# A two-layer streaming encoder on one core: turns between sub-layers by token halves, x on VectorE alone, bias inside the ada dot products

## The chip, the core and the metric

The kernel runs on one core of a Trainium2 chip. The metric is the device time of one execution in microseconds. Three timed runs stand for the kernel before, and one further execution was recorded by the hardware profiler; all durations below come from that one.

## What is computed

544 tokens of width 1024 (512 of a new stream, 32 of a running one) pass through two layers. Each layer has three sub-layers, j = 0, 1, 2: a half-step SwiGLU feed-forward part, a mixer (latent attention beside retention, with one input and one output projection), and a second feed-forward part. Every sub-layer is wrapped in the same way:

```python
mods = silu(c) @ ada_w[l] + ada_b[l]            # 9 vectors of 1024 per layer and stream
h = rms_norm(x, g_pre) * (1 + mods[scale]) + mods[shift]
o = sublayer(h)                                 # swiglu(h @ w1, h @ w3) @ w2, or mixer(h) @ w_out
x = x + coef * mods[gate] * rms_norm(o, g_post) # coef 0.5, 1, 0.5
```

Both norms run over the 1024 features of each token. The outputs are x after both layers, and the new caches and retention states.

## The kernel before

**Layout.** Activations lie feature-major: x is eight rows m = 0 to 7 of 128 features (one per partition) by 544 tokens. A token half is 272 columns, the width of one PSUM bank's use; pair(b) is both halves in banks b and b+1. Every matmul of a projection is done three times with operands split into a high and a low fp32r part: w_hi·h_hi, w_hi·h_lo and w_lo·h_hi (tile3, L668).

**Weights.** SyncE loads a weight chunk into one of two slots of raw, ScalarE casts it to w_hi (high, L1127, and high_at), GpSimd (POOL) subtracts to get w_lo (low, L539), TensorE uses both and counts w_used. A chunk is 1024 columns, or 1408 in the down projection of a feed-forward part, where one output tile needs two chunks (22 k-steps) and there are eight output tiles. The mixer's output tile needs one chunk (8 k-steps). A chunk's cast waits until the chunk two before it, which had the same slot, has been used.

**The ada dot products.** During a down projection VectorE computes mods for the next sub-layers: one tensor_tensor_reduce per tile of 128 outputs and stream (ada_group, L1470), with the tile of ada_w in one of four slots of SBUF and c spread over PSUM banks 4 to 7 (c_psum). There are 48 tiles in a layer's first feed-forward part and 24 in the second (8 in the last layer's), four to a group; a group ends with two additions of the bias (L1486). SyncE's one queue issues these tiles in turn with the down chunks, and each waits for a dot product that frees its slot.

**A turn.** Between two sub-layers each engine's program does this, in order:

- ScalarE, out_tiles (L1225): squares each output tile from PSUM (L1239) and copies it, scaled by gate and gain, to o_buf (L1248, L1250). POOL adds the squares of the tiles up to the seventh (add_square, L545).
- TensorE, at the end of out_tiles: token_sums (L689) multiplies the squares by ones for five groups of tokens, so that each token's sum lies on its own partition; ScalarE takes the root (L1146), VectorE the reciprocal (L1509), TensorE spreads it over all partitions with five transposes (spread, L695).
- VectorE, turn_over (L1504): for each row m a product o·inverse (L1516) and the addition to x (L1520). The additions of rows 1, 3 and 5 are left to POOL (add_odd, L565).
- ScalarE, pre_scale (L1149): h_hi = cast of x·scale for each row (L1157), in two pieces, one for each stream, with the squares of x (L1167) three rows behind. POOL adds the squares of rows 0 to 3.
- VectorE: h_lo for each row (L1550), behind all of x.
- TensorE, first_tiles (L703): the first two output tiles (w = 0, 1) of the next sub-layer. For each row k as it arrives it does the two high products of both tiles and both token halves, 8 matmuls; then, for each w, the products with h_lo, with the sums of squares of x between them (add_squares, L685; five of them).

The order on every engine is written out by hand; semaphores count the steps (x_prod, x_new, h_high, h_ready, sums, sq_added, rooted, inverted, inv_spread, columns, ada_done). At the end of the program the turn has only its first half, and SyncE stores each row of y as x_new counts it (L528). At the start the first turn has only its second half, and takes x from DMA.

## Time and profile before

| | |
|---|---|
| timed runs | median 2369.93 us, 2367.03 to 2370.04 (3 runs) |
| profiled execution | 2367.46 us |
| its span | 2365.7 us |
| TensorE (PE) busy | 2298.3 us |
| VectorE (DVE) busy | 1217.7 us |
| ScalarE (ACT) busy | 807.0 us |
| POOL busy | 907.6 us |
| chain of waits | PE 71%, issue 14%, DVE 8%, DMA 2%, POOL 2%, ACT 1% |

The span runs from the first to the last recorded instruction; the profiled execution's own time is 1.76 us longer. Busy shares are averages over the whole span. Nearly all of it is TensorE streaming through projections; the turns are short stretches in which TensorE's idle time shows only if the profile is asked for that stretch. Starts in a timeline are microseconds from the start of the span. A row with several instructions (x4) gives the time from the first's start to the last's end.

### The profile page before, as it was taken

The page shows a single profiled execution, that of the slowest core. Times are in us where ns is not written, and L with a number is a line of the kernel's source. Part 1 is how long each engine was busy: PE and PEld are TensorE (multiplying, and loading weights), DVE is VectorE, ACT ScalarE, POOL GpSimd, SP SyncE. Part 2 cuts the span into 40 slices and gives each one's busy share as a digit, 9 for nine tenths or more (in the row PEclk, how much of TensorE's full clock was granted, in tenths as well). Part 3 has the DMA queues.
Part 4 walks back from the last instruction along what each step waited for, and adds up shares of the span by engine and source line. Part 5 has one row for each costly group of instructions (what it writes and reads, how often), then busy time and mean ns, then how long its engine had stood idle before and what let it go on. Part 6 is the DMA issues. An engine that isn't in the chain of part 4 may idle for free.

```text
span 2365.7 us, 43949 instructions
## 1 busy us (share of the span) xinstructions
PE 2298.3 (97%) x17664; PEld 2180.3 (92%) x17664; DVE 1217.7 (51%) x2017; ACT 807.0 (34%) x1332; POOL 907.6 (38%) x400
## 2 busy tenths in 40 slices
PE   7999999999999999999999999998999999999997
PEld 7999999899558899999989999998994699999997
DVE  6333379877561533337153333997846524333501
ACT  3322332333454422332242333224343543333321
POOL 2334444434113434434444443444421153443353
PEclk8999999999999999999999999999999999999998
DMA  6222268422211122237212223872231022222421
GB/s 233 89 89 86 83 238 297 143 90 80 73 37 54 63 89 84 85 128 250 103 63 85 83 89 124 279 271 94 81 111 51 1 72 79 82 88 89 162 94 66
DMA packets 70934, 263.62 MB, mean 111 GB/s; under 512 B 8704, under 2 KB 10112, under 8 KB 70336
## 3 DMA queue, kind: packets, MB, share of 16 engines
q1 hardware_dynamic: 70848, 262.44, 32.3%
q8 instruction: 59, 0.97, 0.2%
q14 instruction: 27, 0.22, 0.0%
HBM read 258.96 MB, written 3.45 MB: 111 GB/s over the span
## 4 chain that ended last, share of the span: by engine, by line
PE 71%; issue 14%; DVE 8%; DMA 2%; POOL 2%; ACT 1%; SPq 1%; DVEq 0%; POOLq 0%; ACTq 0%
PE ps L679 20%; PE ps L675 20%; PE ps L676 20%; DVE wide_v L1481 2%; POOL w_lo L542 2%; DMA ada_w<-in_ada 2%; PE ps L685 1%; DVE wide_v L1516 1%; PE ps L725 1%; DVE h_lo L1550 1%; PE ps L1046 1%; DVE x L1520 1%; PE ps L931 1%; DMA x<-in_x 1%; PE ps L1013 1%
## 5 line engine op out<-in xcount | busy, mean ns | idle before, releaser
L542 POOL TENSOR_TENSOR w_lo<-raw,w_hi 128x1024 fp32r<-128x1024 f32 (+1 forms) x304 | 785.2, 2583 | 1278.3 <-ACT w_hi L1139 947.1
L675 PE MATMUL ps<-h_hi,w_hi 128*128 128x272 f32 x3296 | 887.1, 289 | 3.8 <-POOL w_lo L542 3.8
L676 PE MATMUL ps<-h_lo,w_hi 128*128 128x272 f32 x3296 | 889.3, 287 | 0.0
L679 PE MATMUL ps<-h_hi,w_lo 128*128 128x272 f32 x3296 | 685.6, 289 | 0.0
L675 PEld LDWEIGHTS ps<-h_hi,w_hi 128*128 128x128 f32 x3296 | 619.1, 188 | 5.2 <-POOL w_lo L542 5.1
L676 PEld LDWEIGHTS ps<-h_lo,w_hi 128*128 128x128 f32 x3296 | 620.9, 188 | 0.2
L1139 ACT CAST w_hi<-raw 128x1024 fp32r<-128x1024 f32 (+1 forms) x236 | 268.4, 1137 | 831.9 <-PE ps L679 773.9
L679 PEld LDWEIGHTS ps<-h_hi,w_lo 128*128 128x128 f32 x3296 | 519.1, 188 | 0.0
L675 PE MATMUL ps<-u_hi,w_hi 128*128 128x272 f32 x1408 | 380.1, 288 | 0.0
L676 PE MATMUL ps<-u_lo,w_hi 128*128 128x272 f32 x1408 | 379.9, 289 | 0.0
L1481 DVE CUSTOM_DVE_ANT_0 wide_v<-ada_w,ps 128x1024 bf16<-128x1024 f32 x256 | 295.1, 1217 | 27.5 <-DMA ada_w<-in_ada 15.0
L679 PE MATMUL ps<-u_hi,w_lo 128*128 128x272 f32 x1408 | 291.6, 288 | 0.0
L1568 DVE TENSOR_TENSOR wide_v<-ps,rinv 128x544 f32<-128x544 f32 x88 | 63.7, 724 | 437.3 <-PE ps L679 437.3
L675 PEld LDWEIGHTS ps<-u_hi,w_hi 128*128 128x128 f32 x1408 | 264.8, 188 | 0.7 <-POOL w_lo L542 0.7
L676 PEld LDWEIGHTS ps<-u_lo,w_hi 128*128 128x128 f32 x1408 | 265.2, 188 | 0.0
L1573 DVE SCALAR_TENSOR_TENSOR wide_v<-wide_v,wide_s 128x512 f32<-128x512 f32 (+1 forms) x176 | 193.9, 1140 | 104.7 <-ACT wide_s L1211 104.7
L679 PEld LDWEIGHTS ps<-u_hi,w_lo 128*128 128x128 f32 x1408 | 220.3, 188 | 0.0
L1509 DVE RECIPROCAL tok_inv<-tok_root 128x5 f32<-128x5 f32 x6 | 1.1, 188 | 260.8 <-ACT tok_root L1146 260.8
L1214 ACT CAST u_hi<-wide_v 128x544 f32 (+1 forms) x88 | 56.9, 647 | 213.7 <-DVE wide_v L1573 213.7
L1132 ACT CAST w_hi<-raw 128x1024 fp32r<-128x1024 f32 x68 | 71.0, 1045 | 143.6 <-PE ps L679 88.2
L1578 DVE TENSOR_TENSOR u_lo<-wide_v,u_hi 128x544 f32 x88 | 63.9, 726 | 80.1 <-ACT u_hi L1214 80.1
L1211 ACT ACTIVATE wide_s<-wide_s 128x512 f32<-128x512 f32 (+1 forms) x176 | 81.9, 513 | 4.6 <-DVE wide_s L1565 4.6
(257 smaller groups left out, 2390.7 us busy)
## 6 DMA issues: line engine op xcount, KB each, us to landing
raw<-in_w_up SPq DMA_DIRECT2D x176, 512.0 KB, 3.3
ada_w<-in_ada SPq DMA_DIRECT2D x128, 512.0 KB, 4.7
raw<-in_w_dn SPq DMA_DIRECT2D x64, 704.0 KB, 5.4
raw<-in_w_mix SPq DMA_DIRECT2D x64, 512.0 KB, 3.4
ada_first<-in_ada SPq DMA_DIRECT2D x10, 512.0 KB, 7.8
decay<-in_decay SPq DMA_DIRECT2D x2, 2048.0 KB, 10.0
ada_first<-in_ada_first SPq DMA_DIRECT2D x6, 512.0 KB, 11.3
x<-in_x SPq DMA_DIRECT2D x4, 544.0 KB, 16.9
```

The costliest lines, as they stand in the source:

```text
L542: pool.tensor_tensor(w_lo[:, slot, 0:width], raw[:, slot, 0:width], w_hi[:, slot, 0:width].bitcast(F32), ALU.subtract).then_inc(lo_done.se ...
L675: pe.matmul(ps[:, bank + t, 0:width[t]], wh, hi[:, n], start=start, stop=False)
L676: pe.matmul(ps[:, bank + t, 0:width[t]], wh, lo[:, n], start=False, stop=False)
L679: last = pe.matmul(ps[:, bank + t, 0:width[t]], wl, hi[:, n], start=False, stop=stop)
L1132: nc.scalar.copy(w_hi[:, slot, 0:width], raw[:, slot, 0:width]).then_inc(hi_done.sem, 1)
L1139: nc.scalar.copy(w_hi[:, k, 0:width], raw[:, k, 0:width]).then_inc(hi_done.sem, 1)
L1211: nc.scalar.activation(wide_s[:, f, at], wide_s[:, f, at], ACT.Silu, bias=wide_s[:, f, T + 2 * v:T + 2 * v + 1]).then_inc(up_silu.sem, 1)
L1214: nc.scalar.copy(u_hi[:, bass.ds(i * 2 + f, 1), :].rearrange("p a n -> p (a n)"), tmp_v[:, f, :]).then_inc(up_hi.sem, 1)
L1481: v_.tensor_tensor_reduce(junk[v], ada_w[:, t, :], c_psum(v), 1.0, 0.0, ALU.mult, ALU.add, acc[:, buf, v, t:t + 1]).then_inc(ada_done.sem, 1)
L1568: v_.tensor_tensor(halves(tmp_v[:, f, :]), pair(4 * f + 2), halves(rinv[:, :]), ALU.mult)
L1573: v_.scalar_tensor_tensor(out=wide_v[:, f, at], in0=wide_v[:, f, at], scalar=wide_v[:, f, T + 2 * v:T + 2 * v + 1], in1=wide_s[:, f, at], ...
L1578: v_.tensor_tensor(u_lo[:, at, :].rearrange("p a n -> p (a n)"), tmp_v[:, f, :], u_hi[:, at, :].rearrange("p a n -> p (a n)").bitcast(F32) ...
```

## The change

The turns are rewritten.

- **Last output tile.** In every out_tiles the last tile is now done by last_tile: all k-steps of the first 272 tokens, then all of the second 272. Within the second half, at k = 2 TensorE makes the first half's column sums (half_sums(0)), at k = 6 it spreads the first half's inverse (spread(0)). The sums wait for ada_done there. The second half's sums and spread lie in the next sub-layer's first_tiles, within w = 0.
- **x after a feed-forward part** (j = 0, 2). VectorE makes the first token half of all eight rows and then the second. Products go to PSUM banks 6 and 7 instead of SBUF. Nothing is left to POOL.
- **x after the mixer** (j = 1). VectorE makes it in whole rows, products in PSUM banks 6 and 7, each row waiting for the one before.
- **ScalarE.** scaled() takes a token half. After a feed-forward part five rows of the first half are scaled before the last tile's second half is read; the cast of the next chunk stands between. After the mixer both halves of a row follow each other.
- **first_tiles.** The high products of the first token half come first, all rows for w = 0, then all for w = 1; then the second half, row by row, for both.
- **ada.** The dots' loop is written out; the bias is the accumulator's initial value and the result goes straight to mods. The two bias additions per group are gone; columns no longer counts groups.
- **Start.** The first turn scales all rows' first half, then all rows' second.

```diff
...
-TOK_AT = [0, P, 2 * P, 3 * P, T - P]
+TOK_AT = [0, P, HT - P]
 TOK = len(TOK_AT)
...
-SUMS = KD - N_EARLY + 2
+SUMS = KD - N_EARLY + 3
...
-            def add_odd(l, j, m):
-
-                pool.wait_ge(x_prod.sem, x_prod.at(l, j * KD + m + 1))
-                pool.tensor_tensor(x[:, m, :], x[:, m, :], tmp_v[:, 1, :], ALU.add).then_inc(x_new[1].sem, 1)
...
+            def half_sums(l, j, t):
+
+                if t == 0:
+                    pe.wait_ge(sq_added.sem, sq_added.at(l, (j + 1) * SQ))
+                    if j != 1:
+                        pe.wait_ge(ada_done.sem, ada_done.at(
+                            l, 2 * (ADA_A if j == 0 else ADA_A + (ADA_B if l < DEPTH - 1 else KD))))
+                token_sums(squares[:, :], t, True, False)
+                if t:
+                    pe.wait_ge(out_sq.sem, out_sq.at(l, (j + 1) * KD))
+                else:
+                    pe.wait_ge(half_sq.sem, half_sq.at(l, j + 1))
+                token_sums(tmp_s[:, 1, :], t, False, True).then_inc(sums.sem, 1)
+
+            def spread(l, j, t):
+
+                pe.wait_ge(inverted.sem, inverted.at(l, 3 * j + 2 + t))
+                for b in range(2):
+                    c = t * TOK + b
+                    pe.transpose(ps[:, 4 + t, b * P:(b + 1) * P], tok_inv[:, c:c + 1].to_broadcast([P, P]), ident[:, :])
+                c = t * TOK + 2
+                pe.transpose(ps[:, 4 + t, HT - NS:HT], tok_inv[P - NS:P, c:c + 1].to_broadcast([NS, P]),
                              ident[P - NS:P, P - NS:P]).then_inc(inv_spread.sem, 1)
 
...
+                for w in range(2 if l or j else 0):
+                    pe.wait_ge(lo_done.sem, lo_done.at(l, chunk + w + 1))
+                    for k in range(KD):
+                        if w == 0 and k == (0 if j == 2 else 1):
+                            half_sums(*post, 1)
+                        if w == 0 and k == (0 if j == 2 else 5):
+                            spread(*post, 1)
+                        if w == 0:
+                            pe.wait_ge(h_high.sem, h_high.at(l, high_count(l, j, 0, k)))
+                        pe.matmul(ps[:, 2 * w, 0:HT], w_hi[:, w, k * P:(k + 1) * P], h_hi[:, k, 0:HT],
+                                  start=k == 0, stop=False)
+                        pe.matmul(ps[:, 2 * w, 0:HT], w_lo[:, w, k * P:(k + 1) * P], h_hi[:, k, 0:HT],
+                                  start=False, stop=False)
                 for k in range(KD if l or j else 0):
-                    pe.wait_ge(h_high.sem, h_high.at(l, high_count(l, j, k)))
+                    pe.wait_ge(h_high.sem, h_high.at(l, high_count(l, j, 1, k)))
                     for w in range(2):
...
+                        pe.matmul(ps[:, 2 * w + 1, 0:HB], w_hi[:, w, k * P:(k + 1) * P], h_hi[:, k, HT:HT + HB],
+                                  start=k == 0, stop=False)
+                        pe.matmul(ps[:, 2 * w + 1, 0:HB], w_lo[:, w, k * P:(k + 1) * P], h_hi[:, k, HT:HT + HB],
+                                  start=False, stop=False)
...
+            def last_tile(l, j, chunk0, per_tile, chunk_tiles, operand):
+
+                pe.wait_ge(out_ev.sem, out_ev.at(l, j * KD + KD - 2))
+                n0 = chunk0 + (KD - 1) * per_tile
+                last_k = per_tile * chunk_tiles - 1
+                for t in range(2):
+                    n = slice(t * HT, (t + 1) * HT)
+                    for q in range(per_tile):
+                        if t == 0:
+                            pe.wait_ge(lo_done.sem, lo_done.at(l, n0 + q + 1))
+                        for kk in range(chunk_tiles):
+                            k = q * chunk_tiles + kk
+                            if t and k == 2:
+                                half_sums(l, j, 0)
+                            if t and k == 6:
+                                spread(l, j, 0)
+                            hi, lo = operand(k)
+                            slot = (n0 + q) % 2
+                            wh, wl = (w[:, slot, kk * P:(kk + 1) * P] for w in (w_hi, w_lo))
+                            pe.matmul(ps[:, 2 + t, 0:HT], wh, hi[:, n], start=k == 0, stop=False)
+                            pe.matmul(ps[:, 2 + t, 0:HT], wh, lo[:, n], start=False, stop=False)
+                            last = pe.matmul(ps[:, 2 + t, 0:HT], wl, hi[:, n], start=False, stop=k == last_k)
+                        if t:
+                            last.then_inc(w_used.sem, 1)
+                    if t == 0:
+                        last.then_inc(half_mm.sem, 1)
+                if l == DEPTH - 1 and j == 2:
+                    half_sums(l, j, 1)
+                    spread(l, j, 1)
...
+            def scaled(l, j, t, m):
+
+                if l or j:
+                    act.wait_ge(x_new.sem, x_new.at(l, x_count(j - 1, t, m)))
+                elif t == 0:
+                    act.wait_ge(x_in[m // 2].sem, 16)
+                for v, n in ((0, slice(HT, NP_)), (1, slice(NP_, T))) if t else ((0, slice(0, HT)),):
+                    nc.scalar.activation(h_hi[:, m, n], x[:, m, n], ACT.Copy, scale=mul_pre[:, j, v, m:m + 1])\
+                        .then_inc(h_high.sem, 1)
+
...
+            def last_tile(l, j, chunk0, per_tile, o_buf, pre):
+
+                in_u = per_tile == 2
+                ahead = 5 if in_u else 0
+                if pre is not None:
+                    pre_l, pre_j, chunk = pre
+                act.wait_ge(half_mm.sem, half_mm.at(l, j + 1))
+                act.wait_ge(sq_added.sem, sq_added.at(l, j * SQ + N_EARLY + KD - 2))
+                nc.scalar.activation(tmp_s[:, 1, 0:HT], ps[:, 2, 0:HT], ACT.Square).then_inc(half_sq.sem, 1)
+                act.wait_ge(columns.sem, columns.at(l, (2, COL_A, COL_A + 2)[j]))
+                nc.scalar.activation(o_buf[:, KD - 1, 0:HT], ps[:, 2, 0:HT], ACT.Copy,
+                                     scale=mul_post[:, j, 0, KD - 1:KD]).then_inc(half_ev.sem, 1)
+                act.wait_ge(sums.sem, sums.at(l, (j + 1) * SUMS - 1))
+                token_root(0)
+                if pre is not None:
+                    high(pre_l, chunk, 0, KD * P)
+                    if in_u:
+                        shift_columns(pre_l, pre_j)
+                        for m in range(ahead):
+                            scaled(pre_l, pre_j, 0, m)
+
+                act.wait_ge(w_used.sem, w_used.at(l, chunk0 + KD * per_tile))
+                nc.scalar.activation(tmp_s[:, 1, HT:T], ps[:, 3, 0:HT], ACT.Square).then_inc(out_sq.sem, 1)
+                if pre is not None and in_u:
+                    high(pre_l, chunk + 1, 1, KD * P)
+                if pre is not None and not in_u:
+                    shift_columns(pre_l, pre_j)
+                act.wait_ge(sums.sem, sums.at(l, (j + 1) * SUMS))
+                token_root(1)
+                if pre is not None and not in_u:
+                    high(pre_l, chunk + 1, 1, KD * P)
+                n = NP_ - HT
+                nc.scalar.activation(o_buf[:, KD - 1, HT:NP_], ps[:, 3, 0:n], ACT.Copy,
+                                     scale=mul_post[:, j, 0, KD - 1:KD])
+                nc.scalar.activation(o_buf[:, KD - 1, NP_:T], ps[:, 3, n:HT], ACT.Copy,
+                                     scale=mul_post[:, j, 1, KD - 1:KD]).then_inc(out_ev.sem, 1)
+                if pre is not None:
+                    for m in range(ahead, KD if in_u else 0):
+                        scaled(pre_l, pre_j, 0, m)
+                    pre_scale(pre_l, pre_j, chunk)
...
+                        if j == 2:
+                            scaled(l, j, 0, m)
+                        scaled(l, j, 1, m)
...
-            def ada_group(l, buf, land_n, n0, done0, cols, first_ffn=False):
+            def ada_group(l, land_n, n0, done0, first_ffn=False):
+                b0 = l * MODS + 16 + done0
 
                 for t in range(ADA_RING):
                     dve.wait_ge(ada_landed[t].sem, ada_landed[t].at(l, land_n * 16 + 16))
                     if t == 0:
-                        dve.wait_ge(columns.sem, columns.at(l, cols - 2))
-
                         dve.wait_ge(up_lo.sem, up_lo.at(l, FT if first_ffn else 2 * FT))
                         dve.wait_ge(c_placed.sem, c_placed.at(l, 1 if first_ffn else 2))
                     for v in range(2):
                         dve.wait_ge(ada_done.sem, ada_done.at(l, 2 * done0 + (2 * t + v - 1)))
-                        v_.tensor_tensor_reduce(junk[v], ada_w[:, t, :], c_psum(v), 1.0, 0.0, ALU.mult,
-                                                ALU.add, acc[:, buf, v, t:t + 1]).then_inc(ada_done.sem, 1)
-                dve.wait_ge(ada_done.sem, ada_done.at(l, 2 * done0 + 2 * ADA_RING))
-                for v in range(2):
-                    bias = ada_b[:, bass.ds(l * MODS + 16 + done0, ADA_RING)]
-                    v_.tensor_tensor(mods[:, v, bass.ds(n0, ADA_RING)], acc[:, buf, v, :], bias, ALU.add)\
-                        .then_inc(columns.sem, 1)
+                        v_.tensor_tensor_reduce(junk[v], ada_w[:, t, :], c_psum(v), 1.0,
+                                                ada_b[:, b0 + t:b0 + t + 1], ALU.mult, ALU.add,
+                                                mods[:, v, n0 + t:n0 + t + 1]).then_inc(ada_done.sem, 1)
...
+                    def invert(t):
+                        dve.wait_ge(rooted.sem, rooted.at(l, 3 * j + 2 + t))
+                        n = slice(t * TOK, (t + 1) * TOK)
+                        v_.reciprocal(tok_inv[:, n], tok_root[:, n]).then_inc(inverted.sem, 1)
+
+                    if j == 1:
+                        for t in range(2):
+                            invert(t)
+                        dve.wait_ge(inv_spread.sem, inv_spread.at(l, 2 * j + 2))
+                        for m in range(KD):
+                            dve.wait_ge(out_ev.sem, out_ev.at(l, j * KD + m + 1))
+                            c = x_count(j, 1, m)
+                            if m:
+                                dve.wait_ge(x_new.sem, x_new.at(l, c - 1))
+                            v_.tensor_tensor(pair(6), halves(o_buf[:, m, 0:T]), pair(4), ALU.mult).then_inc(x_prod.sem, 1)
+                            dve.wait_ge(x_prod.sem, x_prod.at(l, c))
+                            v_.tensor_tensor(halves(x[:, m, 0:T]), halves(x[:, m, 0:T]), pair(6), ALU.add)\
+                                .then_inc(x_new.sem, 1)
+                    for t in range(2 if j != 1 else 0):
+                        n = slice(t * HT, (t + 1) * HT)
+                        invert(t)
+                        dve.wait_ge(inv_spread.sem, inv_spread.at(l, 2 * j + t + 1))
+                        for m in range(KD):
+                            if t == 0 and m == KD - 1:
+                                dve.wait_ge(half_ev.sem, half_ev.at(l, j + 1))
+                            else:
+                                dve.wait_ge(out_ev.sem, out_ev.at(l, j * KD + m + 1))
+                            c = x_count(j, t, m)
+                            prod = ps[:, 6 + m % 2, 0:HT]
+                            if t or m >= 2:
+
+                                dve.wait_ge(x_new.sem, x_new.at(l, c - 2))
+                            v_.tensor_tensor(prod, o_buf[:, m, n], ps[:, 4 + t, 0:HT], ALU.mult).then_inc(x_prod.sem, 1)
+                            dve.wait_ge(x_prod.sem, x_prod.at(l, c))
+                            v_.tensor_tensor(x[:, m, n], x[:, m, n], prod, ALU.add).then_inc(x_new.sem, 1)
```

## Rows read from the trace of the kernel before

**Rows 1.** The page, busy time by engine: us, share of span, instructions.
```profile
PE 2298.3 (97%) x17664; PEld 2180.3 (92%) x17664; DVE 1217.7 (51%) x2017; ACT 807.0 (34%) x1332; POOL 907.6 (38%) x400
```

**Rows 2.** Waits of TensorE: line, released by, us in total, times, longest.
```profile
PE ps L715 <- ACT h_hi L1157: 9.2, 7, 2.5
...
PE ps L692 <- DVE acc L1481: 2.6, 2, 1.3
```

**Rows 3.** Stretches: start:end, length, each engine's busy us, granted clock, DMA share, GB/s.
```profile
425.30:472.90 47.60, 41.72 (x274) 38.37 (x272) 41.55 (x73) 20.28 (x40) 20.78 (x11) 0.89 0.34 119
767.30:801.60 34.30, 30.25 (x191) 27.76 (x191) 21.26 (x33) 18.91 (x39) 17.59 (x10) 0.90 0.12 39
1171.50:1216.30 44.80, 40.26 (x276) 37.54 (x275) 21.23 (x33) 20.28 (x40) 20.80 (x11) 0.92 0.11 36
1586.50:1632.90 46.40, 40.29 (x273) 37.29 (x272) 41.39 (x73) 20.30 (x40) 20.77 (x11) 0.93 0.35 123
1927.50:1962.20 34.70, 30.66 (x191) 27.97 (x190) 21.23 (x33) 18.91 (x39) 17.58 (x10) 0.85 0.11 37
2332.20:2365.70 33.50, 19.66 (x159) 19.30 (x157) 10.76 (x14) 4.59 (x10) 8.53 (x5) 0.80 0.17 67
```

**Rows 4.** Timeline of VectorE, turn of 1171.5: start, us, instruction, idle before it.
```profile
1191.90 0.72 DVE L1516 TENSOR_TENSOR wide_v<-o_ffn,ps 128x544 f32<-128x544 f32 x1 [0.91 <-PE ps L701]
1192.65 0.72 DVE L1520 TENSOR_TENSOR x<-x,wide_v 128x544 f32<-128x544 f32 x1
...
1201.97 1.14 DVE L1520 TENSOR_TENSOR x<-x,wide_v 128x544 f32<-128x544 f32 x1
...
1203.20 8.88 DVE L1550 SCALAR_TENSOR_TENSOR h_lo<-x,mul_pre,h_hi 128x512 fp32r<-128x512 f32 x16
```

**Rows 5.** Timeline of TensorE, at a tile's start and in the mixer's turn.
```profile
425.34 0.29 PE L675 MATMUL ps<-u_hi,w_hi 128*128 128x272 f32 x1
425.47 0.29 PE L676 MATMUL ps<-u_lo,w_hi 128*128 128x272 f32 x1
...
779.72 0.57 PE L715 MATMUL ps<-h_hi,w_hi 128*128 128x272 f32 x1 [2.58 <-issue]
...
785.31 0.43 PE L717 MATMUL ps<-h_hi,w_lo 128*128 128x276 f32 x1
785.54 0.34 PE L715 MATMUL ps<-h_hi,w_hi 128*128 128x272 f32 x1
...
791.85 0.41 PE L725 MATMUL ps<-h_lo,w_hi 128*128 128x272 f32 x2
```

**Rows 6.** Timeline of ScalarE and POOL: cast and split of chunk 15.
```profile
425.29 1.37 ACT L1139 CAST w_hi<-raw 128x1408 fp32r<-128x1408 f32 x1 [6.91 <-PE ps L679]
426.74 3.24 POOL L542 TENSOR_TENSOR w_lo<-raw,w_hi 128x1408 fp32r<-128x1408 f32 x1 [5.05 <-ACT w_hi L1139]
```

**Rows 7.** Timeline of VectorE in a mixer: 256 columns, one operand in PSUM.
```profile
634.39 0.36 DVE L1711 TENSOR_TENSOR ret_st<-ps,decay 128x256 f32<-128x256 f32 x1
634.67 0.94 DVE L1719 RECIPROCAL ret_root<-ret_root 128x128 f32<-128x128 f32 x1
```

**Rows 8.** Groups of ScalarE by form: count, busy us, mean ns, idle before.
```profile
L1157 ACT ACTIVATE h_hi<-x,mul_pre 128x512 fp32r<-128x512 f32 x48 | 34.2, 713 | 27.2 <-POOL x L568 10.0 <-DVE x L1520 9.2 <-DVE mul_pre L1492 5.5
L1157 ACT ACTIVATE h_hi<-x,mul_pre 128x32 fp32r<-128x32 f32 x48 | 14.7, 306 | 0.0
```

**Rows 9.** Timeline of VectorE: the first dot, then the last group of dots.
```profile
317.18 1.22 DVE L1481 CUSTOM_DVE_ANT_0 wide_v<-ada_w,ps 128x1024 bf16<-128x1024 f32 x1 [1.16 <-ACT ps L1263]
...
433.78 1.22 DVE L1481 CUSTOM_DVE_ANT_0 wide_v<-ada_w,ps 128x1024 bf16<-128x1024 f32 x1 [0.30 <-DVE mods L1486]
...
442.92 0.08 DVE L1481 DVE_READ_ACCUMULATOR2_ANT acc<- 128x1 f32 x1
```

**Rows 10.** The page, DMA issues: queue, count, KB each, median us to landing.
```profile
ada_w<-in_ada SPq DMA_DIRECT2D x128, 512.0 KB, 4.7
...
out_y<-x SPq DMA_DIRECT2D x8, 272.0 KB, 2.1
```

More of the change, by code:

```diff
@@ L277, in streaming_trunk @@
         c_placed = signal("c_placed", 2)
-        x_prod = signal("x_prod", 24)
-        x_new = [signal(f"x_new{i}", 12, 4) for i in range(2)]
+        x_prod = signal("x_prod", 40)
+        x_new = signal("x_new", 40)
         x_sq = signal("x_sq", 24)
@@ L573, in turn_over @@
                     low(l, chunk + k, k, KD * P)
-                if l or j:
-                    for m in range(1, KD - 1, 2):
-                        add_odd(*((l, j - 1) if j else (l - 1, 2)), m)
                 for m in range(1, N_EARLY):
@@ L620, in _ @@
                 ffn(l, 1)
-            for m in range(1, KD - 1, 2):
-                add_odd(DEPTH - 1, 2, m)
         @block.tensor
@@ L687, in add_squares, with token_sums @@
                 return last
-            def token_sums(src, bank, start, stop):
+            def token_sums(src, t, start, stop):
                 for b, at in enumerate(TOK_AT):
-                    last = pe.matmul(by_token(bank)[:, b:b + 1], src[:, at:at + P], ones[:, 0:1],
+                    last = pe.matmul(by_token(t)[:, b:b + 1], src[:, t * HT + at:t * HT + at + P], ones[:, 0:1],
                                      start=start and b == 0, stop=stop, skip_group_check=True)
                 return last
-            def spread(l, n, bank):
-                pe.wait_ge(inverted.sem, inverted.at(l, 2 * n + 2))
-                for b in range(4):
-                    pe.transpose(ps[:, bank, b * P:(b + 1) * P], tok_inv[:, b:b + 1].to_broadcast([P, P]), ident[:, :])
-                pe.transpose(ps[:, bank + 1, 0:NS], tok_inv[P - NS:P, 4:5].to_broadcast([NS, P]),
+            def half_sums(l, j, t):
[10 more added lines that the diff above has]
+                token_sums(tmp_s[:, 1, :], t, False, True).then_inc(sums.sem, 1)
@@ L795, in out_tiles @@
-                pe.wait_ge(out_sq.sem, out_sq.at(l, (j + 1) * KD))
-                token_sums(tmp_s[:, 1, :], 4, False, True).then_inc(sums.sem, 1)
-                spread(l, j, 4)
+                tile(KD - 2, 0, False)
+                last_tile(l, j, chunk0, per_tile, chunk_tiles, operand)
+            def last_tile(l, j, chunk0, per_tile, chunk_tiles, operand):
[26 more added lines that the diff above has]
+                    spread(l, j, 1)
@@ new lines, in shift_columns @@
+            def shift_columns(l, j):
+                act.wait_ge(columns.sem, columns.at(l, COL_A if j else 0))
+                for v in range(2):
+                    c = 3 * j * KD
+                    nc.scalar.copy(h_hi[:, :, T + 2 * v:T + 2 * v + 2],
+                                   mods[:, v, c:c + KD].unsqueeze(2).to_broadcast([P, KD, 2])).then_inc(h_high.sem, 1)
+            def last_tile(l, j, chunk0, per_tile, o_buf, pre):
[36 more added lines that the diff above has]
+                    pre_scale(pre_l, pre_j, chunk)
@@ L1187, in pre_scale @@
                     act.wait_ge(columns.sem, 6)
-                    for m in range(KD):
-                        scaled(m)
-                    shift_columns()
+                    for t in range(2):
+                        for m in range(KD):
+                            scaled(l, j, t, m)
+                    shift_columns(l, j)
                     act.wait_ge(ada_done.sem, 2 * FIRST_TILES)
@@ new lines, in turn_over @@
+                    if j == 1:
+                        for t in range(2):
+                            invert(t)
[9 more added lines that the diff above has]
+                                .then_inc(x_new.sem, 1)
@@ L1833, in mixer @@
                 heads_low(len(ITEMS) - 1)
-            for k in range(KD):
-                v_.memset(scratch[:, 4 + k:5 + k], 0.0).then_inc(x_new[k % 2].sem, 1)
             for v in range(2):
```

165 lines of the change are left out of this document (61 added, 104 removed).

## The prediction

> **What bounds the kernel now.** The page comes first: its busy shares give TensorE 97% of the span [rows 1], so only two things can move the time, TensorE's own work and the places where it stands still. The list of waits, asked for TensorE, says where: at L715 for the scaled activations (ScalarE), at L692 for the ada dot products (VectorE), 2.6 us in two waits [rows 2]. Both lie where one sub-layer's output becomes the next one's input, which I call a turn. There are five between sub-layers and a half one at the end. The table of stretches gives each, from the first matmul of the last output tile to the last matmul of the next sub-layer's first two tiles [rows 3]: 47.6 and 46.4 us for feed-forward to mixer, 34.3 and 34.7 for mixer to feed-forward, 44.8 for feed-forward to the next layer, and 33.5 from the last output tile to the end of the span. TensorE's busy time is 4 to 6 us short of the stretch in each of the five and 14 short in the last, and its clock is below 1.00 in all.
>
> Inside a turn VectorE's timeline shows the order. In the turn of 1171.5 the products and sums that make x run from 1191.90 to 1203.11, then the low parts of h take 8.9 us [rows 4], and TensorE's part on the low parts trails them. That last part of TensorE is 9.8 us long (791.85 [rows 5] to the end of the mixer's turn, 801.6 [rows 3]). So the path is: x on VectorE, h_lo on VectorE, TensorE's last part. I count everything below from the start of the last output tile, as +t.
>
> **Feed-forward turns (three).** The last output tile is 22 k-steps of 6 matmuls, which at full clock follow each other every 0.125 us [rows 5]: 16.5 us. Its first token half now comes first, and needs the second weight chunk after 4.1 us instead of 8.3. That chunk's cast and split take 1.37 and 3.24 us from +0.2 on [rows 6]: it is there at +4.8, 0.7 late. The half ends at +9.1. Two k-steps into the second half TensorE makes six column sums, ScalarE the root, VectorE the reciprocal; at k = 6 TensorE spreads it, until +12.6. The sums are no new work but the old 20 and 5 transposes cut into 12 and 6. The tile ends at +18.6 (before +16.5).
>
> VectorE starts x's first half there, at +12.6. No row has 272 columns with a PSUM destination. The nearest has 256 with a PSUM operand: 0.36 us, the next instruction 0.28 behind it [rows 7]. I take 0.30 for the product and 0.41 for the sum, which waits for it: 0.71 a row, 5.7 us a half, done at +18.3. TensorE sums and spreads the second half by +21.4 (ScalarE casts a chunk in between), so x is whole at +27.1; before it was at +31.6 (1203.11).
>
> Meanwhile TensorE works on the first half of h: w = 0 until +22.5, w = 1 until +24.5. ScalarE scales the second half in two pieces per row and squares whole rows. A 512-column scale is busy for 0.71 and a 32-column one for 0.31 [rows 8]; they overlap by about 0.1, so I take 0.57 for 240 plus 32 columns, 0.38 for 272 and 0.55 for a square. With POOL's three additions between, the last row is scaled at +30.5: ScalarE is last here, not VectorE. TensorE starts on the low parts at +31.0 (before 44.8 - 9.8, +35.0), VectorE has finished them at +36.3, and the turn is through at +40.5. With half operations of 0.36 and 0.46 it is +41.4. I take +40.9: the turns gain 6.7, 5.5 and 3.9 us, 16.1 together.
>
> A rule of the Trainium skill speaks against halving; it stands outside this sum. VectorE: DVE Perf Modes, section on the TRN2 errata, charges every instruction a fixed latency, 120 cycles beside one per element when the source is in PSUM. The 256-column row (0.36 us) has such a fixed part but is shorter. By an estimate from that page a half operation is 0.41 us, and all turns together gain some 3 us less.
>
> **The ada dots.** TensorE's first column sums write a bank that the dots read, so they wait for all dots. Before, they came at +16.5 and waited 1.3 us twice. Now they come at +9.8; the old finish is +17.9 (442.92 + 0.08 [rows 9]). The change takes the bias additions out and unrolls the loop. Eight dots and eight accumulator reads take 9.14 us (433.78 to 442.92), so 96 take 109.7; from 317.18 to 443.00 they took 125.8, and the other 16 us are gaps at 12 group ends. Without gaps VectorE alone would finish at +1.8. But then the queue sets the pace: a down chunk goes out only when the chunk two before it is split, 8.3 us apart, with three ada tiles behind each. With a landing of 4.7 us [rows 10] the last dots are done at +8.2, 1.6 us ahead of need. The column multipliers follow on VectorE and can touch the first reciprocal. The bounds are 0 and +8.1 us in each of two turns; I take 0.5 each, as hardly an old group shows idle time but at its end.
>
> **Mixer turns (two).** The tile is 8 k-steps, 6.0 us; with the interruptions it ends at +7.4. TensorE waits for the next chunk's split (its 1024 columns take 1024/1408 of the cast and split of [rows 6]; +8.3), sums the second half, spreads by +10.3, and only then VectorE makes x in whole rows. Both operations of a row wait for the one before, 0.75 us from start to start [rows 4]: 1.5 us a row, whole at +22.3 against about +21.1. What costs is the new order of first_tiles. TensorE takes the first half of h for w = 0 over all eight rows before anything else, 2 matmuls per 1.5 us, and when the last row is ready (+23.5) 50 of 64 matmuls are still to do, 6.2 us at full clock, to +29.8. Before, each row brought 8 matmuls, and all were done at 791.85 (+24.5). VectorE's low parts (+31.5) hide nothing of it, as TensorE's last part takes 9.2 us more: +39.0, 4.6 worse than before.
>
> The clock comes on top. In the old turn, after 2.6 us without work, matmuls followed each other 0.23 us apart from 779.72 to 785.54, the 1.2 GHz level, and then at 2.4 [rows 5]. In the new one TensorE idles for over two thirds of every row until +23.5, so the burst begins low. If that lasts 5.8 us as there, it costs 0.45 of it, 2.6 us (1 - 0.125/0.227); if the level has come back, nothing. I take 1.6: +40.6, or 6.3 and 5.9 us worse, 12.2 together (bounds 9 and 14.2).
>
> The Trainium skill, TensorE: Matmul & The Clock Gate, section "What's actually happening", has the low level as the default that only activity releases. The old row agrees: 0.23 us apart after the idling. By that rule the burst pays its whole bound, and the sum is 2 us worse.
>
> **The ends.** At the end the second half's sums follow the tile (+18.6), products start at +21.0, the last row is ready at +26.7, and its DMA lands 2.1 us later [rows 10], with 0.5 for eight rows close together: +29.3 against +33.5. Gain 4.2; bounds 2.5 and 4.5. At the start ScalarE scales 24 pieces, 7.4 us, instead of 16, 6.6 us, and the squares wait for it: 0.75 worse, or 0 if a DMA hides it.
>
> **Sum.** -16.1 + 1.0 + 12.2 - 4.2 + 0.75 = -6.4 us. The profiled execution took 2367.46, 1.76 beyond its span, so it gives 2361.1. The three timed runs have a median of 2369.93, 2.5 above it. Midway I expect 2362.
>
> **Rivals.**
> (a) Better: the clock is full when the mixer's burst comes (-3.2), half operations run at 0.28 and 0.36 (-2), no ada wait (-1): 2355. For it: the pitch of 0.28 exists. Against: TensorE's thin work just before the burst.
> (b) Half operations as slow as 0.42 and 0.55, because PSUM is written and read back. Feed-forward turns 42.6, the end 2 us longer, the mixer's x 2 us later each: +5 +2 +4, so 2372, no gain. For it: no row has VectorE writing PSUM. Against: those reading it cost nothing extra (0.36).
> (c) Slower: TensorE waits at the half's sums for the ada dots, two k-steps into the second half of the last tile, twice. It decides from +9.8 on. If landings, not gaps, set the dots' pace, they still end at +17.9, each such turn at +48.6, and the time is 2376. For it: 4.7 us of landing in a ring of four, behind larger chunks on one queue. Against: dots follow each other every 1.14 us within the old groups.
> (d) The bias edit does only half of what it says (the unrolled code brings stalls of its own): dots end at +13.8, +4 us each, 2369, no difference.
>
> **How the numbers follow.** A change under 0.2% (4.7 us) cannot be told from none. Forecast (2357 to 2367) 0.50, (a) 0.13, (b) 0.12, (c) 0.15, (d) 0.10. Faster means below 2365.2: four fifths of the forecast's case, (a) and a little of the rest: 0.60. Slower: (c) and the tail of (b), 0.16. Within: the rest, 0.24. The range runs from (a)'s 2354 to 2372, at (b), and leaves (c) out.
>
> **What would show it.** In the new trace: half operations of x at 0.3 to 0.4 us; feed-forward turns of 40 to 42 us; the last dot before +9.8 and no wait of TensorE for it; mixer turns of 39 to 42 us with the clock low beyond +23.5. I am wrong if the mixer turns are no longer than before, if ada waits of several us stand in two turns, or if the feed-forward turns shrink by less than 3 us.

## The result, and the profile after

The change makes the kernel slower: 2378.53 us (median of 14 runs) against 2369.98 (14 runs), ratio 1.0033 with a 95% interval of 1.0026 to 1.0040. The forecast was 2362. The profiled execution took 2376.92 us; its span is 2375.1, 9.4 more than before. The page gives TensorE the same share as before [rows 1]:

```profile
PE 2306.4 (97%) x17694; PEld 2184.5 (92%) x17694; DVE 1214.2 (51%) x2033; ACT 821.2 (35%) x1392; POOL 880.8 (37%) x382
```

The stretches of the changed kernel, cut as in [rows 3]: three feed-forward turns, two mixer turns and the end, in their order in time.

```profile
427.90:472.00 44.10, 41.54 (x281) 38.75 (x280) 33.00 (x75) 22.42 (x50) 16.05 (x8) 0.92 0.26 90
767.80:809.70 41.90, 32.42 (x196) 28.61 (x195) 21.34 (x37) 21.05 (x49) 12.93 (x7) 0.80 0.10 31
1180.00:1223.60 43.60, 40.47 (x281) 37.40 (x280) 23.91 (x53) 22.41 (x50) 16.05 (x8) 0.96 0.12 37
1593.80:1636.90 43.10, 40.14 (x280) 37.46 (x279) 33.23 (x75) 22.41 (x50) 16.06 (x8) 0.96 0.26 92
1931.30:1973.40 42.10, 32.61 (x196) 28.81 (x195) 21.33 (x37) 21.05 (x49) 12.93 (x7) 0.80 0.09 33
2343.70:2375.10 31.40, 20.85 (x164) 20.04 (x162) 13.34 (x34) 5.04 (x12) 4.51 (x2) 0.86 0.19 72
```

Set against the lengths of [rows 3] and the terms of the prediction's sum:

| term | predicted | in the trace |
|---|---|---|
| start (first last-tile at 427.9, before 425.3) | +0.75 | +2.6 |
| three feed-forward turns | -16.1 | -3.5, -1.2, -3.3 = -8.0 |
| wait for the dots | +1.0 | 0 |
| two mixer turns | +12.2 | +7.6, +7.4 = +15.0 |
| end | -4.2 | -2.1 |
| between the turns | 0 | +1.9 |
| sum | -6.4 | +9.4 |

The last column compares one profiled execution of each kernel. Every turn moved the way that was forecast, but nearly every size is off, and all but one (the wait for the dots) to the slow side. TensorE's waits (line waited for, released by, us, times, longest) show where:

```profile
PE ps L730 <- ACT h_hi L1203: 16.1, 16, 2.1
PE ps L737 <- ACT h_hi L1203: 6.7, 11, 1.4
...
PE ps L688 <- POOL w_lo L548: 1.8, 2, 0.9
```

L730 is the first token half's high product in first_tiles: 8 of its 16 waits lie in each mixer turn, one per row. No wait for the dots is left [rows 2]: the last dot ends 8.6 us into the first turn (forecast +8.2), 1.3 us before the column sums that need it (+9.9), though each now takes 1.20 us from start to start instead of 1.14 [rows 9]. VectorE at the last dot:

```profile
435.16 1.30 DVE L1563 CUSTOM_DVE_ANT_0 wide_v<-ada_w,ps,ada_b 128x1024 bf16<-128x1024 f32 x1
436.36 0.11 DVE L1563 DVE_READ_ACCUMULATOR2_ANT mods<- 128x1 f32 x1
```

**A feed-forward turn.** From VectorE's timeline in the first turn: product, sum and next product of x's second half, then the low parts.

```profile
450.46 0.45 DVE L1618 TENSOR_TENSOR ps<-o_ffn,ps 128x272 f32<-128x272 f32 x1 [1.02 <-PE ps L713]
450.94 0.44 DVE L1620 TENSOR_TENSOR x<-x,ps 128x272 f32<-128x272 f32 x1
451.29 0.44 DVE L1618 TENSOR_TENSOR ps<-o_ffn,ps 128x272 f32<-128x272 f32 x1
...
457.84 8.86 DVE L1649 SCALAR_TENSOR_TENSOR h_lo<-x,mul_pre,h_hi 128x512 fp32r<-128x512 f32 x16
```

An operation behind an unrelated one starts 0.35 us after it, the sum behind its own product 0.48: 0.83 a row (forecast 0.71), 6.7 us a half. x is whole at +29.3 (forecast +27.1), h_lo done at 466.70, +38.8 (+36.3). The last row is scaled at +32.3 (460.24; forecast +30.5):

```profile
459.55 0.69 ACT L1203 ACTIVATE h_hi<-x,mul_pre 128x240 fp32r<-128x240 f32 x2
```

**A mixer turn.** TensorE's granted clock is the column behind POOL's busy time:

```profile
781.00:793.20 12.20, 5.75 (x14) 3.51 (x14) 11.25 (x17) 10.32 (x27) 4.00 (x4) 0.50 0.14 45
793.20:796.40 3.20, 3.16 (x14) 3.16 (x15) 3.20 (x7) 1.80 (x4) 1.42 (x1) 0.50 0.00 0
796.40:801.10 4.70, 4.70 (x38) 4.70 (x38) 4.05 (x10) 0.00 (x0) 0.00 (x0) 0.99 0.00 0
801.10:809.70 8.60, 8.60 (x54) 7.80 (x53) 1.04 (x1) 3.09 (x4) 2.39 (x1) 1.00 0.00 0
```

The four stretches are the rows, the burst behind the last row in two parts, and the low parts. TensorE follows VectorE's rows with 2 matmuls each, at 1.2 GHz and busy for 5.75 of 12.2 us. The first half of the last row is ready at 793.2 (+25.4); 50 matmuls follow, 3.2 us of them at 1.2 GHz, to 801.1: 7.9 us.

### The profile page after: what moved, and what is told of

The parts are those of the page before. It is cut to its first block, busy times and chain, and to the rows that moved or that the text cites. A ratio compares the mean times of both kernels' runs of the same rounds, so it can differ in the third digit from the quotient of the medians.

```text
span 2375.1 us, 43827 instructions
## 1 busy us (share of the span) xinstructions
PE 2306.4 (97%) x17694; PEld 2184.5 (92%) x17694; DVE 1214.2 (51%) x2033; ACT 821.2 (35%) x1392; POOL 880.8 (37%) x382
## 3 DMA queue, kind: packets, MB, share of 16 engines
q1 hardware_dynamic: 70848, 262.44, 33.2%
## 4 chain that ended last, share of the span: by engine, by line
PE 75%; issue 10%; DVE 5%; POOL 4%; ACT 3%; DMA 1%; SPq 1%; POOLq 0%; DVEq 0%; ACTq 0%
PE ps L675 20%; PE ps L671 20%; PE ps L672 20%; POOL w_lo L548 4%; DVE wide_v L1563 2%; PE ps L681 1%; PE ps L747 1%; PE ps L1092 1%; PE ps L834 1%; PE ps L835 1%; PE ps L836 1%; PE ps L977 1%; DMA x<-in_x 1%; PE ps L1059 1%; PE ps L1115 1%
## 5 line engine op out<-in xcount | busy, mean ns | idle before, releaser
L671 PE MATMUL ps<-u_hi,w_hi 128*128 128x272 f32 x1232 | 332.7, 288 | 1.0 <-POOL w_lo L548 1.0
L672 PE MATMUL ps<-u_lo,w_hi 128*128 128x272 f32 x1232 | 332.4, 289 | 0.0
L1563 DVE CUSTOM_DVE_ANT_0 wide_v<-ada_w,ps,ada_b 128x1024 bf16<-128x1024 f32 x256 | 308.9, 1287 | 21.7 <-DMA ada_w<-in_ada 17.2
L675 PE MATMUL ps<-u_hi,w_lo 128*128 128x272 f32 x1232 | 255.1, 288 | 0.0
L671 PEld LDWEIGHTS ps<-u_hi,w_hi 128*128 128x128 f32 x1232 | 231.7, 188 | 1.9 <-POOL w_lo L548 1.9
L672 PEld LDWEIGHTS ps<-u_lo,w_hi 128*128 128x128 f32 x1232 | 232.1, 188 | 0.0
L675 PEld LDWEIGHTS ps<-u_hi,w_lo 128*128 128x128 f32 x1232 | 192.8, 188 | 0.0
```

The lines of the kernel that those rows point to most:

```text
L671: pe.matmul(ps[:, bank + t, 0:width[t]], wh, hi[:, n], start=start, stop=False)
L672: pe.matmul(ps[:, bank + t, 0:width[t]], wh, lo[:, n], start=False, stop=False)
L675: last = pe.matmul(ps[:, bank + t, 0:width[t]], wl, hi[:, n], start=False, stop=stop)
L1563: v_.tensor_tensor_reduce(junk[v], ada_w[:, t, :], c_psum(v), 1.0, ada_b[:, b0 + t:b0 + t + 1], ALU.mult, ALU.add, mods[:, v, n0 + t:n0 + ...
```

## The experiments

Ratios are to the kernel before, run beside each. Differences in us are differences of ratios times 2370. The intervals reach 2 to 3 us to either side, so smaller differences are read from the turns in the traces. The edits are given in short, not line by line. "Theory 1" and "Theory 2" are those of the expectation that stands above each result.

**mixer_rows: the changed kernel, the old order in the mixer turns.**

```diff
-  w = 0: first half, 8 rows (sums, spread at k = 0); w = 1 likewise; then second half, both w
+  if j == 2: half_sums(1); spread(1)
+      for k: wait for both halves of row k; for w, for t: w_hi*h_hi, w_lo*h_hi
```

> The changed kernel, but in the two mixer turns TensorE takes the high products row by row again (8 matmuls when both halves of a row are scaled). Theory 1 (the order of first_tiles is what costs there): in the trace of the changed kernel the last row is ready 25.4 us into the turn and 50 matmuls, 7.9 us, follow it; row by row only 8 follow, 1.8 us at 1.2 GHz, so each turn is 6 us shorter, less 0.5 to 1.5 us if the clock is still low when the low parts begin: 2378.5 - 9 to 12 = 2367 to 2369.5, and mixer turns of 36 to 37.5 us. Theory 2 (the clock sets the price, not the order): TensorE is still at 1.2 GHz through the low parts, which then take 11 to 12 us instead of 8.6, and each turn is shorter by 3 us at most: 2372.5 or more.

2366.86 us, ratio 0.9988 (0.9979 to 0.9997), so 10.7 us under the changed kernel. The two mixer turns, and in the first of them the high products and the low parts:

```profile
765.90:802.80 36.90, 30.74 (x196) 27.52 (x195) 21.35 (x37) 21.01 (x49) 12.92 (x7) 0.91 0.11 38
1927.20:1964.40 37.20, 30.89 (x197) 27.27 (x196) 21.41 (x37) 21.01 (x49) 12.91 (x7) 0.91 0.11 37
780.30:793.20 12.90, 11.12 (x66) 10.24 (x66) 12.07 (x18) 10.74 (x27) 4.47 (x3) 0.85 0.14 42
793.20:802.80 9.60, 9.40 (x53) 7.85 (x52) 6.40 (x15) 3.31 (x5) 2.39 (x1) 1.00 0.00 0
```

Theory 1. TensorE is back at 2.4 GHz 3.9 us after its first matmul, long before the last row; each row now brings 8 matmuls. One loop carries more than the whole loss of 8.5 us: with it undone the change is a little faster than the kernel before (0.7 to 5 us by the interval). 2.6 and 2.5 us a turn remain against before [rows 3].

**order_alone: the kernel before, with the new order in the mixer turns.**

```diff
-  for k: wait for row k; for w, for t: w_hi*h_hi, w_lo*h_hi
+  if j == 2: w = 0, then w = 1: first token half, 8 rows (w = 0 waits for each);
+             then the second token half, both w
```

> The kernel before with one edit: in the two mixer turns TensorE takes the high products in the changed kernel's order (w = 0 and w = 1 of the first token half, then the second half). x, its scaling and everything else stay. Theory 1 (the order leaves 50 of 64 matmuls behind the last row, and TensorE starts on them at 1.2 GHz): what follows the last row grows from 1.8 to 6.5 to 8 us, each mixer turn from 34.4 to 39 to 40.5 us, 2370 + 9 to 12 = 2379 to 2382, ratio 1.004 to 1.005. Theory 2 (what costs in the changed kernel is that x is made later by VectorE alone): 2 us at most, 1.001.

2382.97 us, ratio 1.0070 (1.0056 to 1.0084). The mixer turns:

```profile
766.20:807.40 41.20, 32.78 (x193) 29.24 (x192) 21.22 (x33) 18.90 (x39) 17.51 (x10) 0.75 0.10 32
...
1933.50:1974.70 41.20, 32.78 (x193) 29.23 (x191) 21.20 (x33) 18.90 (x39) 17.51 (x10) 0.75 0.10 34
```

6.9 and 6.5 us more than in [rows 3], with x made as before. The starts are reckoned back from the column sums, 6.2 us; counted from the sums themselves it is 6.8 and 6.3. The order costs this by itself: Theory 1, and a little over its upper end (40.5 us a turn, ratio 1.005).

**bias_only: the kernel before with the bias in the dots.**

```diff
-  tensor_tensor_reduce(junk, ada_w, c, 1.0, 0.0, ..., acc); per group: mods = acc + ada_b
+  tensor_tensor_reduce(junk, ada_w, c, 1.0, ada_b[...], ..., mods), groups unrolled
```

> The kernel before with one edit, the bias as a term of the ada dot product (and the loop over groups written out). Theory 1 (the edit is sound, the loss lies in the turns and at the start): the two feed-forward turns that follow first feed-forward parts lose their 1.3 us wait of TensorE for the dots, 2369.98 - 2.6 = 2367.4. Theory 2 (the dots are part of the loss: each takes 1.20 us from start to start in the changed kernel, 1.14 before, and their earlier end starts the transfers of the next chunks elsewhere): no faster, or slower by up to 2 us, 2370 to 2372. The last dot should end 7 to 9 us after the start of the last output tile instead of 17.9.

2367.2 us, ratio 0.9988 (0.9979 to 0.9997): 2.8 us faster, Theory 1, though the interval (0.7 to 5 us) is wide for it. TensorE's list of waits has no row for the dots. The last dot,

```profile
436.65 1.28 DVE L1480 CUSTOM_DVE_ANT_0 wide_v<-ada_w,ps,ada_b 128x1024 bf16<-128x1024 f32 x1
```

ends some 10.4 us into the turn, 1.4 later than the end of the expected range, and later than the changed kernel's sums at +9.9 (the tile's start is reckoned back by 16.5 us from its column sums at 444.0).

**old_start: the changed kernel with the old pieces at the start.**

```diff
-  for t, for m: scaled(0, 0, t, m)       # 272; then 240 and 32 columns
+  for m: 512 columns, 32 columns
```

> The changed kernel, with ScalarE scaling the very first x in two pieces a row (512 and 32 columns) as before. Theory 1: the changed start is 0.96 us late at the last shift column (40.15 against 39.19) and that is all that the edit costs by itself; the other 1.6 us of the 2.5 come from the clock, which is at 1.2 GHz from 49.6 to 52.5 us after the longer wait. If the clock follows the longer wait, both go: 2376.0. Theory 2: the low clock there is chance and not the edit's; then 2377.5.

2376.83 us, ratio 1.0030 (1.0017 to 1.0042): 0.7 us under the changed kernel, which the intervals cannot tell from none. The clock from 40 to 58 us, in old_start and then in bias_only, which also has the old start:

```profile
40.00:58.00 18.00, 15.51 (x106) 14.51 (x105) 6.05 (x9) 11.50 (x15) 8.01 (x5) 1.00 0.10 29
```

```profile
40.00:58.00 18.00, 15.65 (x94) 14.21 (x94) 4.47 (x11) 10.41 (x14) 6.40 (x4) 0.91 0.00 1
```

bias_only reaches its first dot at 319.66, to the hundredth where the changed kernel does, with the old scaling at the start. The other profiles say the same: the first last output tile starts at 425.4 in old_start and 425.5 in sums_start, at 426.0 to 426.2 in the six other kernels with the new start, and at 427.9 in the changed kernel alone. So the traces speak for Theory 2, which the times can't tell from Theory 1: the edit costs 0.5 to 1.0, as forecast, and the rest of the 2.6 us belongs to the execution that was profiled. That the clock is what made it late there is not shown: x_pairs had a mean of 0.83 in the same stretch and still began its last output tile at 426.2.

**sbuf_products: half products in SBUF.**

```diff
-  prod = ps[:, 6 + m % 2, 0:HT]
+  prod = tmp_v[:, m % 2, 0:HT]
```

> The changed kernel, with the products of the half rows of x written to SBUF instead of PSUM. Theory 1 (writing and reading back PSUM is what makes a half operation 0.44 us where I had estimated 0.30 and 0.41): 0.36 us each and a row in 0.70 instead of 0.83, a half in 5.7 instead of 6.7 us; three feed-forward turns and the end are shorter by 1 to 2 us each: 2372 to 2375. Theory 2 (it is the 272 columns and the wait of each sum for its product): the same 0.44 us and 0.83 a row, 2378.5.

2384.69 us, ratio 1.0062 (1.0048 to 1.0075), 6.9 us over the changed kernel. Theory 2 for the single operations, neither for the time: the three feed-forward turns are 1.5, 3.1 and 3.1 us longer. VectorE, then POOL, in the first turn:

```profile
442.86 0.43 DVE L1618 TENSOR_TENSOR wide_v<-o_ffn,ps 128x272 f32<-128x272 f32 x1
443.33 2.17 DVE L1620 TENSOR_TENSOR x<-x,wide_v 128x272 f32<-128x272 f32 x1
...
447.54 2.48 DVE L1620 TENSOR_TENSOR x<-x,wide_v 128x272 f32<-128x272 f32 x1
```

```profile
442.77 2.44 POOL L548 TENSOR_TENSOR w_lo<-raw,w_hi 128x1024 fp32r<-128x1024 f32 x1 [10.38 <-ACT w_hi L1178]
447.36 2.37 POOL L548 TENSOR_TENSOR w_lo<-raw,w_hi 128x1024 fp32r<-128x1024 f32 x1 [2.15 <-ACT w_hi L1178]
```

The operations are no shorter (0.43, 0.44), so PSUM was not what made them 0.44. But a sum that meets a POOL split of 2.4 us now lasts until the split ends (442.77 + 2.44 = 445.21; the sum ends at 445.50), while the product ahead of it, with one operand in PSUM, took 0.43 under the same split. In the changed kernel the same split (444.47, 2.41) lies under sums of 0.44 whose product is in PSUM. This is a benefit of the change that I had not seen. The Trainium skill, SBUF — State Buffer, section "SBUF: two separate sides", states the rule: a VectorE instruction with two SBUF inputs and a GpSimd instruction that reads SBUF take one pair of ports as an exclusive lock, for the whole instruction. The trace agrees: 2.17 and 2.48 us for sums that otherwise take 0.44.

**x_pairs: mixer_rows, and no sum right behind its product.**

```diff
-  for m: product(m), sum(m)
+  feed-forward: product(m), product(m+1), sum(m), sum(m+1)
+  mixer: product(first half of m), product(second), sum(first), sum(second)
```

> On top of mixer_rows (0.9988 of before), the operations that make x are put in pairs: product, product, sum, sum, all of 272 columns, so that no sum stands right behind its own product; in the mixer turn the pair is the two halves of one row. Theory 1 (a dependent sum starts 0.12 us later than an independent one): operations 0.35 to 0.36 us apart, a half row in 0.71 instead of 0.83 and a mixer row in 1.42 instead of 1.59. The mixer turns go from 37 to 35.5 us, the end is 1 us shorter, the feed-forward turns lose little, as ScalarE is last there: 2.5 to 4.5 us together, 0.9970 to 0.9978 of before. Theory 2 (the spacing is VectorE's own for 272 columns): 0.42 us apart whatever the order, and the mixer turns grow to 38 us.

2361.13 us, ratio 0.9964 (0.9950 to 0.9977). VectorE:

```profile
448.74 0.80 DVE L1633 TENSOR_TENSOR ps<-o_ffn,ps 128x272 f32<-128x272 f32 x2 [1.02 <-PE ps L713]
449.44 0.78 DVE L1637 TENSOR_TENSOR x<-x,ps 128x272 f32<-128x272 f32 x2
450.14 0.79 DVE L1633 TENSOR_TENSOR ps<-o_ffn,ps 128x272 f32<-128x272 f32 x2
```

Four operations in 1.40 us: 0.35 each, 0.70 a row. The turns:

```profile
426.20:469.20 43.00, 40.26 (x281) 37.58 (x280) 32.88 (x75) 22.24 (x50) 16.65 (x8) 0.96 0.27 94
765.20:801.10 35.90, 30.64 (x196) 27.62 (x195) 21.38 (x53) 20.96 (x49) 12.94 (x7) 0.90 0.12 39
```

Theory 1. The first two feed-forward turns gained about 1 us each too, against mixer_rows, which I had not expected: TensorE was not simply waiting for ScalarE, whose last row came only 0.3 us earlier (+32.0). The third is 1.2 us longer (44.4 against 43.2), for there TensorE waited at the half's sums for the last dot, which ended at +11.6:

```profile
PE ps L688 <- DVE mods L1578: 1.6, 1, 1.6
```

This is rival (c)'s wait, once and small. The 1.3 us of room in the changed kernel do not hold in every execution: old_start and sums_start have such a wait of 0.2 us each.

**squares_behind: mixer_rows, with ScalarE's squares of x moved behind its scalings.**

```diff
-  scaled(m); if m >= 3: squared(m - 3)
+  scaled(m); if m in (3, 4): squared(m - 3)      # the rest after all rows
```

> On top of mixer_rows, ScalarE squares only rows 0 and 1 of x between its scalings; rows 2 to 7 are squared when all of h_hi is done. Theory 1 (in the feed-forward turns ScalarE sets the path: its last row is ready 32.3 us into the turn, 3 us after x is whole, and two squares and a 0.9 us wait for POOL stand ahead of it): the last row is ready at 30.5 and the turn is 1 to 2 us shorter, three times; 0.9970 to 0.9978 of before. Theory 2: the squares are then late for TensorE, which sums them between its low parts, and the turns stay or grow: 0.9988 or more.

2367.44 us, ratio 0.9986 (0.9975 to 0.9997), level with mixer_rows. The high products of the feed-forward turns end at +31.0 instead of +33.2 to 33.6, 2.4 us earlier, yet the turns take 43.8, 43.0 and 43.0 us where mixer_rows took 44.0, 44.0 and 43.2. The edit holds in the mixer turns too, and they grew from 36.9 and 37.2 to 37.9 and 37.8 us, so that the whole time shows neither. TensorE's waits now, over all turns:

```profile
PE ps L762 <- DVE h_lo L1664: 4.7, 5, 1.4
PE ps L681 <- ACT wide_s L1278: 3.8, 3, 1.4
```

Theory 2 for the time. What is last is no longer ScalarE's rows but h_lo and the squares. As the edit itself made the squares late, it does not show what the turn would gain from earlier rows alone.

**mixer_shared: mixer_rows, with the mixer's x in SBUF and POOL taking three sums, as before.**

```diff
-  ps product of a whole row, sum on VectorE, for all 8 rows
+  tmp_v product; sums of rows 1, 3 and 5 on POOL
```

> On top of mixer_rows, the mixer turn's x is made as in the kernel before: products in SBUF, the sums of rows 1, 3 and 5 on POOL. Theory 1 (POOL's share is worth having: two rows in 2.64 us in the kernel before, 3.18 on VectorE alone): the mixer turns go from 37 to 35 us, 0.9970 of before. Theory 2 (sums with both operands in SBUF and POOL's instructions keep each other out, so that sharing gives nothing): no gain, 0.9988.

2367.25 us, ratio 0.9988 (0.9978 to 0.9998). Both mixer turns take 38.0 us, 1 more than in mixer_rows. Theory 2, with a price: VectorE's first sum stands under POOL's split (775.53 to 777.87),

```profile
776.18 2.27 DVE L1630 TENSOR_TENSOR x<-x,wide_v 128x544 f32<-128x544 f32 x1
```

The kernel before makes that split earlier (from 775.28, x from 777.17). The change cast the second chunk later and so put the split beneath x; once that is so, VectorE alone with PSUM products gives the shorter turn; the whole times are level.

**sums_first and sums_start.** sums_first is x_pairs with the mixer turn's second column sums freed from the wait for the next split (L688 <- POOL w_lo in the list above); sums_start adds old_start.

```diff
   if j == 2:
-      wait for lo_done(chunk)
       half_sums(1); spread(1)
```

> On top of x_pairs (0.9964 of before): in the mixer turn TensorE makes the second half's column sums without waiting for the next chunk's split. Theory 1: the tile ends at +8.1 and the sums start at +9.0, so x and all behind it come 0.9 us earlier, twice: 1.8 us, 0.9956. Theory 2 (ScalarE, which stands between with a root, a square and a cast, is late anyway): under 0.5 us each, 0.9962.

> sums_first and the start as before (first x scaled in two pieces a row). From old_start (0.7 us, by its ratio) and the changed kernel's trace (0.96 us at the last shift column): 0.7 to 1 us under sums_first, 0.9953. If the clock dip at 49.6 to 52.5 us of the changed kernel belonged to the edit, it would be 2.5.

2359.58 us, ratio 0.9960 (0.9947 to 0.9974), and 2358.89 us, 0.9965 (0.9952 to 0.9979). sums_first's mixer turns:

```profile
764.90:799.80 34.90, 30.57 (x196) 27.98 (x195) 21.40 (x53) 20.95 (x49) 12.93 (x7) 0.90 0.13 41
1922.20:1957.10 34.90, 30.55 (x197) 27.91 (x195) 21.43 (x53) 20.94 (x49) 12.93 (x7) 0.90 0.11 40
```

1.0 and 1.3 us shorter than in x_pairs: Theory 1 in the trace; the whole time cannot show it. The start's 0.7 us stays unresolved in the times (the ratio even moves the other way). Either kernel beats the one before by about 9 us and the changed one by 16 to 17.

## Why the prediction was wrong

**What held.** The bound (x, then h_lo, then TensorE's last part), the dots (+8.6 against +8.2, and bias_only's 2.8 us fits their two old waits of 2.6 [rows 2]), the first half's end (+9.2 against +9.1), the start's own cost (0.5 to 1.0), and the cause in the mixer turn: 50 matmuls behind the last row, 7.9 us against 6.2 + 1.6. The clock came back 3.2 us into them and cost 1.7, not the whole bound of 2.6. Rivals (c) and (d), the dots late, did not come true in the changed kernel; x_pairs shows how near (c) was.

**The step that failed: the feed-forward turns, "the turns gain 6.7, 5.5 and 3.9 us, 16.1 together".** They gained 8.0, and the middle one only 1.2, which the prediction had named as a sign of being wrong. Half of the whole miss of 15.8 us is this term. Inside it, "0.30 for the product and 0.41 for the sum ... 0.71 a row" was mis-sized: 0.35 and 0.48, 0.83 a row. I had scaled the nearest row (256 columns, 0.36 [rows 7]) down instead of taking it as the lower end. That is 1.0 us a half. The Trainium skill's VectorE: DVE Perf Modes, section on the TRN2 errata, by which I had estimated 0.41 for a half operation, was nearer: an operation is 0.44 in the rows, and two of 0.41 would make 0.82 a row. The second half of x began at +22.6, forecast +21.4; 0.8 of that was already there when the tile ended (+19.4 against +18.6). Together x was whole 2.2 us late, in all three turns, and h_lo and TensorE's last part moved with it. The rest of the miss, 1.0, 0.5 and 0 us, lies in that last part: its clock had been 1.00 in all three old turns and was 0.81, 0.84 and 0.89 in the new ones, which the sum had left out. In the first it took 10.6 us, after TensorE had waited for rows:

```profile
461.40:472.00 10.60, 10.60 (x54) 9.42 (x54) 6.40 (x14) 3.75 (x5) 2.68 (x2) 0.81 0.00 0
```

**"The last row is scaled at +30.5: ScalarE is last here, not VectorE"** does not hold as the turn's bound. The row came at +32.3. squares_behind took 2 us from it and the turns shortened by 0.2, 1.0 and 0.2 only; x_pairs took 0.3 from it and 1 us from x on VectorE, and the two turns without a wait for dots shortened by 1.0 and 1.2. So the path runs through h_lo at least as much as through ScalarE's rows. How the rest is shared between h_lo, the squares and the clock is not shown.

**The mixer turns** cost 15.0, against 12.2 and bounds of 9 to 14.2. The order is worth 10 (mixer_rows) to 13.4 (order_alone) of it; order_alone has another x and another clock (0.75 against 0.80). The rest is x: it starts at +11.7 and a row takes 1.59 us, where I had 1.5 from [rows 4]; a next product that waits for the sum starts 0.82 behind it, not 0.75.

**The end** gained 2.1 of 4.2: two halves at 6.7 us and sums later. **Between the turns** 1.9 us were lost; 1.4 of them in the first mixer, where the same work ran at a mean clock of 0.91 (before 0.94). The change touches nothing there. order_alone, whose mixers are the old ones, spends 1.6 us more between the turns in the second layer than in the first, with the same work, so a step of this size needs no change of the mixer. That it is chance in the changed kernel is not shown.

```profile
619.00:699.00 80.00, 75.22 (x469) 39.49 (x470) 58.08 (x113) 33.33 (x76) 13.88 (x9) 0.91 0.12 38
```

Rival (b) had the direction of the operations right; its excess of 0.26 us a row was twice the real 0.12. The slower side was left to (c), one late wait, where it came from four terms (the feed-forward turns, the mixer turns, the end, the start), each too favourable, and from what was lost between the turns. The range ended at (b)'s 2372 and held none of their sum. Two small slips in the working change nothing: (a) is 2355 in its own sum and 2354 in the range, and the dots without gaps would end at +1.6, not +1.8.

## What to carry to other kernels

When work arrives in rows, give the consumer all that a row allows as it arrives: work kept back for a later loop is paid in full behind the last row, and at TensorE's low clock if the rows left it idle. Splitting an operation in two costs some fixed time again (two halves of 272 columns take 0.70 us from start to start, where 544 took 0.65 in the kernel before), and a consumer right behind its producer costs more (0.48 against 0.35); put an independent instruction between them. Leave a margin for what an engine must have ready: 1.3 us of room was gone in one turn of x_pairs. A net gain that is the difference of two large terms (-16 and +12 here) needs a range built from errors of both, and a part that loses can be tried without the rest.

## What the runs showed of the hardware

- VectorE, 272 columns of fp32: 0.44 us, next start 0.35 us later if independent, 0.48 if it waits for the result; the same with the product in PSUM or SBUF.
- A VectorE sum with both operands in SBUF that meets a POOL split of a weight chunk lasts until that ends (2.17 and 2.48 us instead of 0.44); with one operand in PSUM it does not.
- An ada dot with a bias read as its start value: 1.28 to 1.30 us, and 1.20 from start to start, against 1.22 and 1.14 without.
- With 2 matmuls per 1.59 us TensorE stayed at the 1.2 GHz level for 12 us and for 3.2 us of the burst behind; in mixer_rows, with 8 per row, it was back at 2.4 GHz 3.9 us after its first matmul.
